# Two layers of a hybrid backbone on one core: opening on three queues, the last two items' rows added by 0/1 products, and expert gates applied to result rows

## The chip, the core and the metric

The kernel runs on one core of one Trainium2 chip: TensorE (PE) multiplies, VectorE (DVE) and ScalarE (ACT) work on tiles, GpSimd (POOL) and SyncE (SP) issue transfers, and so can ScalarE. 16 DMA engines move data between HBM and SBUF. The metric is the time of one execution on the device, in microseconds.

## What is computed

256 context rows and 256 latent rows of 1024 floats (f32) pass two layers; the output is the 256 latent rows, normed. The reference in short:

```python
for i in range(2):
    mod_l = split(silu(c) @ w_mod[i] + b_mod[i], 6)      # six vectors of 1024 for latent rows; mod_c for context rows
    u = modulated_norm(x, norm1_w[i], mod[0], mod[1]) @ w_in[i]
    y = token_mixers(u)                                  # SSD, Hyena long convolution, mLSTM, side by side
    x = x + mod[2] * (y @ w_out[i])
    x = x + mod[5] * hier_moe(modulated_norm(x, norm2_w[i], mod[3], mod[4]))
return rmsnorm(xl, final_norm_w)

def hier_moe(h):     # 4 groups of 8 experts: each row goes to 2 experts of its best group
    hid = silu(h @ w_gate[e]) * (h @ w_up[e]);  out += weight * (hid @ w_down[e])
```

Each expert has three matrices of 1 MB. In layer 1 only the latent rows go through the experts, in layer 0 all 512 rows.

## The kernel before

The program is one list of instructions per engine, written by hand; `due(name)` is the semaphore value at which a named step is done. x lies in SBUF as four tiles of 128 rows (0, 1 context, 2, 3 latent), PSUM has eight banks, given out in turn by `product`.

**Opening.** SP issues everything: the condition vectors and `ident`, the Hyena filter's parameters, then the weights of modulation in eight parts of 1 MB (three pairs, `first_pair`, and two single ones, `first_single`, numbers 6 and 7), x between them, the biases `b_mod`, the norm weights; then the in-projection's weights through a ring of four slots of 1 MB (`weight`), with `parameters(0)` (some 45 small loads), `router_parameters(0)` and constants in between. Modulation vectors 0 and 1 need parts 0 to 7: PE multiplies a part, ACT copies it to `grow`, PE transposes it (`mod_vector`), DVE sums it (`mod_columns`), then `modulators` writes `ab`. The filter of the Hyena convolution is made in six steps (`filter_step` 0 to 5) that stand between these. PE transposes the normed input (`input_columns`), ACT (context) and DVE (latent) scale it into `hT`, and the in-projection (`channel_major`, first "hy") starts when all of `hT` and the small columns (`pcol`) are there. The gates' product (`gate_sums`) comes after the six "hy" blocks.

**Experts.** Behind the router each expert's rows form items of up to 64 rows: 33 items in layer 0, 32 in layer 1. For item j, POOL gathers rows from DRAM (`rows`), PE transposes them (`gathered`), multiplies by gate and up (`gate_up`), ACT and DVE form the hidden rows, PE transposes (`hidden`) and multiplies (`down`). The 64x1024 result stands in one bank, the second half of its columns in partitions 64 to 127. In layer 0 ACT scales it by each row's weight (`weighted`) and the gate vector mod[5] is applied at the start of layer 1; in layer 1 DVE scales and gates it at once (`gated_halves`). POOL scatters it to `pair_rows` in DRAM, where each row of x has two places. Weights come to 17 (18) places of 1 MB (`expert_slots`), each reloaded when its matrix is used. A loop for more items (`flag != 0`) isn't entered with these inputs.

**Boundary.** All engines wait for each other (`stage_end`). SP waits for the last scatters and loads the pair rows of tiles 2, 3, 0, 1; DVE adds the two places (`pair_sum`), multiplies by the gate (`pair_gate`, layer 0) and adds to x (`pair_add`). Then come square (ACT), inverse (DVE), root (ACT), scaling, transposes and the in-projection of layer 1. Behind layer 1 the same sums lead to the output norm (`normed_output`).

## Time and profile before

| | |
|---|---|
| three runs | 1328.37, 1325.08, 1327.77 us; median 1327.77 |
| profiled execution | 1324.55 us, of which the span is 1322.6 us |
| PE busy | 1170.5 us (88%) |
| DVE, ACT, POOL busy | 605.8, 305.9, 133.2 us |
| DMA | 323.50 MB, mean 245 GB/s |

Times below are microseconds from the start of the span. Busy times of engines overlap, so shares don't add up to the whole. What counts is which engine or transfer the others wait for in a stretch.

### The profile page before, as it was taken

Reading aid. Unit: us, or ns where it says so; the run is one execution under the profiler, and the core shown is the slowest. Engines: PE = TensorE matmul, PEld = TensorE weight load, DVE = VectorE, ACT = ScalarE, POOL = GpSimd, SP = SyncE. Lnnn points to the kernel's source line nnn. Section 1 sums busy time; section 2 is a strip of 40 time slices with the busy share of each in tenths; the row PEclk is TensorE's granted clock in tenths of the full one; section 3 lists DMA queues with packets and bytes.
Section 4 is the critical chain, followed back from the end, with each engine's and each line's share of the span. In section 5 each row is a group of like instructions: output and inputs, shape, how many; then the busy total and the mean of one; then the engine's idle time right before and its main releaser. Section 6 shows DMA issues by size and latency. Waiting matters only on the chain. (4 is left out here: it accounts for less than half of the span.)

```text
span 1322.6 us, 19488 instructions
## 1 busy us (share of the span) xinstructions
PE 1170.5 (88%) x7596; PEld 769.2 (58%) x7596; DVE 605.8 (46%) x1233; ACT 305.9 (23%) x623; POOL 133.2 (10%) x144
## 2 busy tenths in 40 slices
PE   6799999999899979999877689998889899988882
PEld 3444547987678855555444466467768655545551
DVE  4424996037973641343111266973393533332223
ACT  4201112254552202131111233141442100000001
POOL 0000000000000012222221100000000112221220
PEclk9799999998999979999898899998999899998997
DMA  8653233236663579999999755441484879999982
GB/s 289 194 163 98 94 111 96 86 123 198 205 243 101 234 249 384 391 388 376 374 385 387 268 188 166 127 139 49 159 273 189 345 306 388 386 389 390 403 340 113
DMA packets 146965, 323.50 MB, mean 245 GB/s; under 512 B 28249, under 2 KB 111254, under 8 KB 121912
## 3 DMA queue, kind: packets, MB, share of 16 engines
q1 hardware_dynamic: 135384, 306.17, 63.8%
q0 software_dynamic: 11392, 15.79, 3.7%
q8 instruction: 63, 1.03, 0.3%
q14 instruction: 30, 0.25, 0.1%
q10 hardware_dynamic: 96, 0.26, 0.0%
HBM read 321.37 MB, written 22.28 MB: 260 GB/s over the span
## 5 line engine op out<-in xcount | busy, mean ns | idle before, releaser
L657 PE MATMUL bank<-hT,ring 128*128 128x512 f32 (+1 forms) x544 | 207.9, 540 | 1.8 <-DVE hT L1784 1.8
L657 PE MATMUL bank<-ring,hT 128*128 128x256 f32 (+1 forms) x928 | 180.3, 349 | 8.7 <-DVE chain L1794 3.9
L657 PEld LDWEIGHTS bank<-ring,hT 128*128 128x128 f32 x928 | 154.3, 194 | 27.8 <-issue 7.2
L657 PEld LDWEIGHTS bank<-hT,ring 128*128 128x128 f32 x544 | 104.5, 194 | 98.9 <-issue 91.9
L1788 DVE TENSOR_TENSOR ktok<-ktok,bank 64x256 f32<-64x256 f32 x65 | 27.5, 423 | 278.2 <-ACT ktok L1401 198.0
L657 PE MATMUL bank<-chain,qkT 128*64 128x256 f32 (+1 forms) x760 | 138.8, 380 | 6.1 <-DMA chain<-in_moe_w_up 2.7
L1401 ACT ACTIVATE ktok<-bank 64x256 f32<-64x256 f32 (+2 forms) x79 | 32.1, 406 | 346.9 <-PE bank L657 295.0
L657 PE MATMUL bank<-ring,qkT 128*64 128x256 f32 x512 | 92.7, 409 | 15.8 <-DMA ring<-in_moe_w_up 7.7
L1334 POOL DMA_INDIRECT pair_rows<-hyT,ysum x65 | 65.7, 1011 | 382.5 <-ACT hyT L1401 194.9
L657 PEld LDWEIGHTS bank<-chain,qkT 128*64 128x64 f32 (+1 forms) x760 | 82.6, 150 | 26.1 <-issue 4.8
L657 PEld LDWEIGHTS bank<-ring,qkT 128*64 128x64 f32 x512 | 56.3, 147 | 33.4 <-issue 15.1
L1401 ACT ACT_TABLE_LOAD x33 | 42.3, 1283 | 112.1 <-PE bank L657 68.5
L657 PE MATMUL bank<-big,qkT 128*64 128x256 f32 x256 | 60.3, 390 | 7.5 <-DMA chain<-in_moe_w_up 3.0
L1329 POOL DMA_INDIRECT big<-h_rows,ysum x65 | 61.7, 950 | 47.2 <-DVE ysum L1788 28.0
L1343 POOL DMA_DIRECT2D grow<-in_b_mod x4 | 2.3, 584 | 593.0 <-ACT grow L1401 593.0
L1214 PEld LDWEIGHTS bank<-ident,big 64*128 64x128 f32 x520 | 37.5, 140 | 37.3 <-issue 26.4
L657 PE MATMUL bank<-ident 128*128 128x256 f32 x188 | 51.4, 430 | 8.6 <-DMA hT<-pair_rows 7.7
L1794 DVE COPY qkT<-bank 128x512 f32<-128x512 f32 x65 | 45.0, 692 | 25.1 <-PE bank L1214 23.3
L1214 PE MATMUL bank<-ident,big 64*128 64x64 f32 x520 | 46.1, 229 | 9.8 <-DMA big<-h_rows,ysum 7.6
L657 PE MATMUL bank<-hT,qkT 128*64 128x256 f32 x256 | 51.0, 406 | 2.6 <-DMA hT<-in_moe_w_up 1.7
L1237 PEld LDWEIGHTS bank<-ident,ktok 64*128 64x128 f32 x130 | 20.3, 204 | 55.0 <-DVE qkT L1794 36.5
L1788 DVE TENSOR_TENSOR big<-big,bank 128x384 f32<-128x384 f32 x48 | 26.6, 554 | 55.5 <-ACT big L1401 52.1
(298 smaller groups left out, 1748.1 us busy)
## 6 DMA issues: line engine op xcount, KB each, us to landing
ring<-in_w_mod SPq DMA_DIRECT2D x40, 1024.0 KB
ring<-in_w_in SPq DMA_DIRECT2D x22, 1024.0 KB
chain<-in_moe_w_up SPq DMA_DIRECT2D x21, 1024.0 KB
chain<-in_moe_w_gate SPq DMA_DIRECT2D x19, 1024.0 KB
ring<-in_moe_w_down SPq DMA_DIRECT2D x18, 1024.0 KB
chain<-in_moe_w_down SPq DMA_DIRECT2D x17, 1024.0 KB
ring<-in_moe_w_gate SPq DMA_DIRECT2D x16, 1024.0 KB
ring<-in_moe_w_up SPq DMA_DIRECT2D x16, 1024.0 KB
```

Source lines behind the costliest of these rows:

```text
L657: return nc.tensor.matmul(o, a, b, start=s, stop=e, **k)
L1214: last = nc.tensor.transpose(b[:, k * R:(k + 1) * R], rows_v[r0:r0 + R, j % 2, k * P:(k + 1) * P], ident[r0:r0 + R, r0:r0 + R])
L1237: last = nc.tensor.transpose(b[:, f * R:(f + 1) * R], hid_v[0:R, j % 2, f::2], ident[0:R, 0:R])
L1329: return nc.gpsimd.indirect_dma_start(dst, None, h2_rows, bass.IndirectOffsetOnAxis(at_, 0), bounds_check=NT * P - 1, oob_is_err=False)
L1334: return nc.gpsimd.indirect_dma_start(pair_halves, bass.IndirectOffsetOnAxis(at_, 0), src, None, bounds_check=2 * MOST_PAIRS - 1, oob_is_e ...
L1343: pool.dma_start(modrow(m)[2:3, :], A["b_mod"][l:l + 1, m * D:(m + 1) * D]).then_inc(gate_bias_in[l][n], tick(f"gate_bias{l}{n}_in", ("gat ...
L1401: step(nc.scalar.activation(o, i, f, **k), *names)
L1788: step(V.tensor_tensor(o, a, b, op), *names)
L1794: step(V.tensor_copy(o, a), *names)
```

## The change

1. Opening on three queues. SP issues `ident`, the condition vectors, x, the eight parts and the in-projection's weights, nothing else. ACT issues the parameters of the filter's first steps. POOL issues the rest: 17 loads at once, and 38 after part 7 has been used. The small columns have their own semaphore (`prow`), and the "hy" block 0 waits for each k of `hT` apart. Filter steps 4 and 5 move behind the first two "hy" blocks.
2. Row gates. Layer 0's gate vector is applied to each item's result rows on DVE, by a row gate made of the context's and the latent rows' gate (two operations per item); `gate_rows(1)` stands in the router's stage in both layers; `pair_gate` and `weighted` are gone.
3. Late rows. The latent rows of the last two items are not scattered: PE adds them up into two banks per tile by a 0/1 matrix (`late`, `late_rows`), and DVE adds the banks to x (`pair_late`). So the pair rows of tiles 2 and 3 are loaded behind the scatter of the third-last item. The places in DRAM that aren't written are set to zero first (`zero_pairs`), and two of the weight places aren't reloaded late, as the pair rows are loaded there. `stage_end` behind the experts becomes a mark for each engine alone.

```diff
+LATE_ITEMS = 2
+PAIR_PLACES, LAST_IN_PAIRS = ((4, 5), (14, 4)), 80
 def taken_again(l, s, n):
+    if s in PAIR_PLACES[l] and n > LAST_IN_PAIRS:
+        return False
...
@@ SP @@
                 if l == 0:
-                    fetch("cond_in", cond_v[:, :, 0], A["c"][0].rearrange("(p k) -> p k", k=KB))
-                    fetch("cond_in", cond_v[:, :, 1], A["c_ctx"].rearrange("(p k) -> p k", k=KB))
-                    fetch("cond_in", ident[:, :], A["const_ident"])
-                    hidden_parameters(0)
-                    tap_parameters(0)
+                    fetch(sp, "cond_in", ident[:, :], A["const_ident"])
...
+                    fetch(sp, "x_in", x_v[:, 0:2, :], A["ctx"][0].rearrange("(t p) d -> p t d", p=P))
...
                     first_pair(0)
...
                     first_pair(1)
                     first_pair(2)
-                    fetch("dft_in", dft[:, :], A["const_dft"])
                     first_single(6)
-                    for layer in range(DEPTH):
-                        fetch("mod_bias_in", bmod_v[:, layer], A["b_mod"][layer].rearrange("(m p k) -> p m k", m=6, k=KB))
-                    norm_weights(0)
                     first_single(7)
...
+                if l:
+                    for t in (2, 3):
+                        sp.wait_ge(*due(("pairs", l - 1, t)))
+                zero_pairs(f"zeros{l}_in")
...
+                for n in (2, 1):
+                    sp.wait_ge(*due(("scattered", l, EXPERTS + EXTRA[l] - LATE_ITEMS - n)))
+                for t in (2, 3):
+                    sp.wait_ge(*due(last_in(PAIR_PLACES[l][t - 2])))
+                    sp.dma_start(two_v[l][t], pair_tiles[t]).then_inc(
+                        pairs_in[t], tick(f"pairs{t}_in", ("pairs", l, t), by=16))
...
-                for n in (1, 2):
-                    sp.wait_ge(*due(("scattered", l, EXPERTS + EXTRA[l] - n)))
...
+                if l + 1 < DEPTH:
+                    for n in (2, 1):
+                        sp.wait_ge(*due(("scattered", l, EXPERTS + EXTRA[l] - n)))
+                    for t in (0, 1):
+                        sp.dma_start(two_v[l][t], pair_tiles[t]).then_inc(
...
@@ PE @@
                         for k in range(KB):
+                            if (name, blk) == ("hy", 0):
+                                for s in range(1 if a0 else 0, 2):
+                                    pe.wait_ge(*due(("h1T", l, s, k)))
...
+                    if l == 0 and q == 0:
+                        pe.wait_ge(*due(("four",)))
+                        filter_step(l, 4)
+                        filter_step(l, 5)
...
-                if l:
-                    gate_rows(1)
+                gate_rows(1)
...
+                def late(t):
+
+                    b = [product(("late", l, t, half)) for half in range(2)]
+                    pe.wait_ge(*due(("late hot", l)))
+                    for n in range(LATE_ITEMS):
+                        j = items_now - LATE_ITEMS + n
+                        pe.wait_ge(*due(("result", l, j)))
+                        for half in range(2):
+                            rows = slice(R * half, R * half + R)
+                            last = mm(b[half][:, :], late_hot[l][rows, n, t - 2, :], res_v[rows, j % 2, :],
+                                      n == 0, n == LATE_ITEMS - 1)
...
@@ POOL @@
+            fetch(pool, "taps0_in", tcol[:, :], A["const_tcol"])
+            tap_parameters(pool, 0)
...
+            mod_biases(0)
+            norm_weights(pool, 0)
+            fetch(pool, "dft_in", dft[:, :], A["const_dft"])
+            parameters(pool, 0)
+            pool.wait_ge(*due(("made", ("mod", 0, 7))))
+            gate_parameters(pool, 0)
+            mod_biases(1)
...
+            router_parameters(pool, 0)
...
@@ DVE @@
-            def pair_gate(l, t):
-                two = two_v[l][t]
-                tt(two[:, 0, :], two[:, 0, :], grow_v[:, t // 2, :], MUL)
+            def pair_late(l, t):
+
+                dve.wait_ge(*due(("made", ("late", l, t))))
+                for half in range(2):
+                    cs_ = slice(512 * half, 512 * half + 512)
+                    tt(x_v[:, t, cs_], x_v[:, t, cs_], bank(("late", l, t, half))[:, :], ADD,
...
+                    if l and n == 0:
+                        step(V.memset(big[:, 0:2048], 0.0))
...
+                    ts(row_gate[:, j % 2, :], gate_halves[0], context_of[:, j:j + 1], None, MUL, None)
+                    stt(row_gate[:, j % 2, :], gate_halves[1], latent_of[:, j:j + 1], row_gate[:, j % 2, :], MUL, ADD)
...
+                    if l == 0:
+                        row_gates(j)
-                    if l and j:
+                    if j:
                         gated_halves(j - 1)
...
+                pair_sum(l, 2)
+                gated_halves(items_now - 1)
+                pair_add(l, 2)
+                pair_late(l, 2)
+                pair_sum(l, 3)
+                pair_add(l, 3)
+                pair_late(l, 3)
```

The order on PE in the opening, before: `four,ysum` is filter step 4, `tables` step 5, `xtok,condp` and `chain,condp` are parts 6 and 7, `ident,big` the transposes of the input, `hT,ring` the in-projection.

```order
L657 MATMUL bank<-hT,condp 32x256 x16
L657 MATMUL bank<-four,ysum 128x1 x4
L657 MATMUL bank<-qkT,tables 128x512 x2
L657 MATMUL bank<-hyT,tables 128x512 x2
L657 MATMUL bank<-xtok,condp 32x256 x8
L657 MATMUL bank<-chain,condp 32x256 x8
L688 MATMUL bank<-ident,grow 128x128 x8
L771 MATMUL bank<-ident,big 128x128 x32
L764 MATMUL bank<-ident,prow 128x78
L657 MATMUL bank<-hT,ring 128x512 x16
```

The same place in the changed program:

```order
L682 MATMUL bank<-xtok,condp 32x256 x8
L682 MATMUL bank<-chain,condp 32x256 x8
L713 MATMUL bank<-ident,grow 128x128 x8
L789 MATMUL bank<-ident,big 128x128 x32
L682 MATMUL bank<-hT,ring 128x512 x8
L782 MATMUL bank<-ident,prow 128x78
L682 MATMUL bank<-hT,ring 128x512 x8
L682 MATMUL bank<-ring,condp 32x256 x8
L682 MATMUL bank<-four,ysum 128x1 x4
L682 MATMUL bank<-qkT,tables 128x512 x2
L682 MATMUL bank<-hyT,tables 128x512 x2
L682 MATMUL bank<-hT,ring 128x512 x16
```

Steps 4 and 5 have moved from ahead of part 6 to behind the first two blocks of the in-projection, and the small columns (`ident,prow`) behind its first block.

DVE behind the last item of layer 1, before (`hyT<-bank,ysum,grow` is the scaled and gated result):

```order
L1788 TENSOR_TENSOR big<-big 128x1024
L1788 TENSOR_TENSOR x<-x,big 128x1024
L1788 TENSOR_TENSOR hT<-hT 128x1024
L1784 TENSOR_SCALAR small<-small 128x1
L1842 RECIPROCAL small<-small 128x1
L1788 TENSOR_TENSOR x<-x,hT 128x1024
L1791 SCALAR_TENSOR_TENSOR big<-x,small,ktok 128x1024
```

DVE there in the changed program:

```order
L1847 TENSOR_TENSOR big<-big 128x1024
L1850 SCALAR_TENSOR_TENSOR hyT<-bank,ysum,grow 128x512
L1847 TENSOR_TENSOR x<-x,big 128x1024
L1847 TENSOR_TENSOR x<-x,bank 128x512 x2
L1847 TENSOR_TENSOR hT<-hT 128x1024
L1847 TENSOR_TENSOR x<-x,hT 128x1024
L1847 TENSOR_TENSOR x<-x,bank 128x512 x2
```

The first sum of pair rows (`big<-big`) now stands ahead of the last item's result, each tile has two sums from banks more, and the inverse of tile 2 (`small`) comes behind all of them instead of behind the sum of tile 3.

## Rows read from the trace of the kernel before

**Rows 1.** Windows: busy us of each engine in the stretch, granted PE clock, DMA share, GB/s.

```profile
37.00:38.00 1.00, 1.00 (x8) 0.82 (x8) 0.93 (x3) 0.20 (x1) 0.00 (x0) 1.00 0.14 22
...
59.00:64.00 5.00, 4.86 (x7) 2.25 (x8) 0.24 (x1) 0.00 (x0) 0.00 (x0) 0.50 1.07 352
60.00:110.00 50.00, 50.00 (x162) 21.58 (x162) 14.14 (x19) 2.35 (x5) 0.00 (x0) 0.95 0.53 167
600.00:700.00 100.00, 84.58 (x586) 47.79 (x582) 21.02 (x42) 12.79 (x24) 22.98 (x24) 0.95 1.02 378
...
1294.00:1295.00 1.00, 1.00 (x13) 0.78 (x11) 0.00 (x0) 0.00 (x0) 0.00 (x0) 1.00 0.06 25
```

**Rows 2.** Timeline of SP's DMA issues, opening: start, duration, what is loaded.

```profile
24.69 10.01 SPq L401 DMA_DIRECT2D bmod<-in_b_mod  x2
...
37.54 0.55 SPq L482 DMA_DIRECT2D chain<-in_w_mod  x1
...
55.72 0.43 SPq L401 DMA_DIRECT2D rb<-in_exp_router_b  x1
```

**Rows 3.** Timeline of PE, opening: start, duration, operation, [idle before <-releaser].

```profile
36.63 1.05 PE L657 MATMUL bank<-four,ysum 128*128 128x1 f32 x8
...
41.15 1.07 PE L657 MATMUL bank<-xtok,condp 128*32 128x256 f32 x16
44.74 1.93 PE L657 MATMUL bank<-chain,condp 128*32 128x256 f32 x16 [2.52 <-DMA chain<-in_w_mod]
...
59.14 0.37 PE L764 MATMUL bank<-ident,prow 78*128 78x78 f32 x1 [5.18 <-DMA rb<-in_exp_router_b]
59.38 16.65 PE L657 MATMUL bank<-hT,ring 128*128 128x512 f32 x32
...
91.89 14.00 PE L657 MATMUL bank<-hT,ring 128*128 128x512 f32 x32
...
107.99 2.37 PE L657 MATMUL bank<-hT,tables 128*64 128x512 f32 x10
```

**Rows 4.** Timelines of PE, DVE, POOL and SP at the boundary of the layers.

```profile
742.30 1.94 PE L657 MATMUL bank<-big,ysum 128*64 128x512 f32 x8 [0.57 <-DVEq L1319]
...
767.81 8.83 PE L657 MATMUL bank<-hT,ring 128*128 128x256 f32 x32 [1.82 <-DVE hT L1784]
...
753.59 1.23 DVE L1788 TENSOR_TENSOR hT<-hT 128x1024 f32<-128x1024 f32 x1 [7.25 <-DMA hT<-pair_rows]
...
735.84 1.00 POOL L1334 DMA_INDIRECT pair_rows<-hyT,ysum  x1 [6.85 <-ACT hyT L1401]
...
748.61 0.91 SPq L628 DMA_DIRECT2D hT<-pair_rows  x2
```

**Rows 5.** Timelines of PE, DVE and POOL at the end of the span.

```profile
1298.48 1.94 PE L657 MATMUL bank<-hT,ysum 128*64 128x512 f32 x8 [0.98 <-DVE ysum L1794]
...
1300.55 0.75 DVE L1791 SCALAR_TENSOR_TENSOR hyT<-bank,ysum,grow 128x512 f32<-128x512 f32 x1 [2.22 <-PEq L668]
...
1317.80 1.28 DVE L1791 SCALAR_TENSOR_TENSOR big<-x,small,ktok 128x1024 f32<-128x1024 f32 x1 [0.77 <-ACT small L1401]
...
1291.81 1.00 POOL L1334 DMA_INDIRECT pair_rows<-hyT,ysum  x1 [5.86 <-DVE ysum L1794]
```

**Rows 6.** Timeline of DVE, opening: the latent half of the scaled input.

```profile
50.23 6.18 DVE L1784 TENSOR_SCALAR hT<-bank,ab 128x256 f32<-128x256 f32 x8
```

**Rows 7.** Groups of POOL by line: busy us, mean ns, idle before.

```profile
L1347 POOL DMA_DIRECT2D h_rows<-big x6 | 3.3, 544 | 146.9 <-ACT big L1401 146.9
```

**Rows 8.** Timeline of PE in the router's stages of layers 0 and 1.

```profile
465.89 1.09 PE L657 MATMUL bank<-qkT,hyT 128*128 128x47 f32 x8 [0.38 <-DVE qkT L1788]
...
1040.87 1.08 PE L657 MATMUL bank<-grow,gate_four 128*64 128x512 f32 x4
```

**Rows 9.** Landings of scatters issued in 600:700, and of the one in 1291:1292.5.

```profile
DMA to landing us min/median/max: 6.8/7.3/8.1
...
DMA to landing us min/median/max: 3.9/3.9/3.9
```

More of the change, by code:

```diff
@@ L182, in build @@
         consts_in, x_in, norm_in, out_written = sem("consts_in"), sem("x_in"), sem("norm_in"), sem("out_written")
+        prow_in = [sem(f"prow{l}_in") for l in range(DEPTH)]
         params_in = [sem(f"params{l}_in") for l in range(DEPTH)]
@@ L197, in build @@
         more_rows_out = [sem(f"more_rows{l}_out") for l in range(DEPTH)]
+        zeros_in = [sem(f"zeros{l}_in") for l in range(DEPTH)]
+        more_zeros = [sem(f"more_zeros{l}_in") for l in range(DEPTH)]
+        more_pairs = [sem(f"more_pairs{l}_in") for l in range(DEPTH)]
+        more_sums = [sem(f"more_sums{l}") for l in range(DEPTH)]
         more_weights = [sem(f"more_weights{l}_in") for l in range(DEPTH)]
@@ L225, in build @@
         rw = sb("rw", KB * 36)
+        steps = sb("steps", 72)
         rb = sb("rb", 36)
@@ L601, in _, with last_in @@
                     sp.wait_ge(*due(("more table", l)))
-                    fetch("norm_in", final_w, A["final_norm_w"].partition_broadcast(P))
+                    fetch(sp, "norm_in", final_w, A["final_norm_w"].partition_broadcast(P))
+                def last_in(s):
+                    return ("used", ("expert", l, max(n for n in range(matrices) if places[n] == s)))
+                for n in (2, 1):
[4 more added lines that the diff above has]
+                        pairs_in[t], tick(f"pairs{t}_in", ("pairs", l, t), by=16))
                 if l + 1 < DEPTH:
@@ L1271, in _ @@
                 down(items_now - 1)
-                stage_end(l, "moe")
+                for t in (2, 3):
+                    late(t)
+                pe.drain().then_inc(pe_done, tick("pe_done", ("end", "pe", l, "moe")))
                 with pe.If(flag != 0):
+                    pe.wait_ge(*due(("end", "act", l, "moe")))
+                    pe.wait_ge(*due(("end", "dve", l, "moe")))
                     pe.nop().then_inc(more_pe[l], 1)
@@ L1357, in rows @@
                         rows_in[j % 4], tick(f"rows{j % 4}_in", ("rows", l, j), by=16))
+                pool.wait_ge(*due((f"zeros{l}_in",)))
                 for j in range(AHEAD):
@@ L1478, in _ @@
                     act.wait_ge(*due(("ab", l, 0)))
-                    for k in range(0, KB, 2):
-                        input_columns(k, 1, ("h1T", l, 1, "act"))
+                    for blk in (0, 2):
+                        name = ("h1", l, blk, 1)
+                        act.wait_ge(*due(("made", name)))
+                        for k in (2 * blk, 2 * blk + 1):
+                            names = [("read", name)] if k % 2 else []
+                            fn(hT_v[:, k, L:2 * L], bank(name)[:, 256 * (k % 2):256 * (k % 2) + L], ACT.Identity, *names,
+                               ("h1T", l, 1, k), scale=ab_v[:, 0, k, 0:1], bias=ab_v[:, 1, k, 0:1])
                     input_squares(0)
@@ L1914, in _ @@
                     step(V.memset(vaug[:, :], 1.0))
-                    for n in (1, 2, 3):
-                        filter_step(l, n)
+                    filter_step(l, 1)
+                    inverse(l, 0, NT)
+                    filter_step(l, 2)
                 def normed_input(t):
```

401 lines of the change are left out of this document (214 added, 187 removed).

## Prediction

> **What bounds the kernel now.** I read the windows first. In the window from 60 to 110 us PE is busy for 50.00 of 50 us [rows 1]: once the in-projection runs, PE is the bound and nothing beside it costs time. In the window from 600 to 700 PE is busy for 84.58 us, while the DMA engines stand at a share of 1.02 and 378 GB/s [rows 1]: a mixture-of-experts stage is bound by its 3 MB of weights per item (3.15 MB / 378 GB/s = 8.3 us), and VectorE with 21.02 us has room. Three places are left where neither is full, and the change works at them.
>
> The opening: SP issues everything. The two bias loads hold it for 10.01 us from 24.69, so weight part 7, the last that the first norm's modulators need, is issued only at 37.54 [rows 2]; between 37 and 38 us the DMA engines move 22 GB/s [rows 1]. PE takes part 7 at 44.74, and the in-projection starts at 59.38, behind a wait of 5.18 us that ends with the router's bias, issued at 55.72 as the last of some 50 small parameters [rows 2, 3].
>
> The boundary of the layers: the last product of the last item starts at 742.30 and takes 1.94, so ends at T = 744.24; in-projection of layer 1 starts at 767.81 [rows 4], 23.6 us later. Between them lie the scaled result, its scatter, the load of the pair rows (issued at 748.61, awaited by VectorE until 753.59, so 5.0 us), and sums of 1.23 us.
>
> The end: the last product starts at 1298.48 and ends at T' = 1300.42; the output norm's last operation starts at 1317.80 [rows 5], and the span ends at 1322.6, 22.2 us after T'.
>
> **The change, part by part.**
>
> *Opening, gain.* SP now issues three small loads (about 0.7 us each), the five of x, then the weight parts with nothing between them. Up to the end of part 7 these are 8.4 MB of parts, 2.1 MB of x, and beside them about 1.1 MB on the other two queues (filter weights, decays, the Fourier table). 11.6 MB at 378 to 390 GB/s are 30 to 31 us; they can flow from about 5 us, so part 7 is there at 36, and PE takes it at about 36.5 instead of 44.74: 8.2 earlier. From there to the modulators it took 5.5 us (44.74 to the first use at 50.23 [rows 3, 6]); I keep it, so 42.1. Next, before, PE waited until all 16 blocks of the normed input were scaled and then for the parameters: 59.38 - 50.23 = 9.15. Now each product waits for its own k, and the parameters aren't asked for. But PE must first issue 32 transposes into 8 banks, two for each k, and VectorE frees a pair of banks every 6.18 / 8 = 0.77 us [rows 6]; so it can start after about five of them, 3.9 us. In-projection then starts at 46.0: 13.4 earlier.
>
> *Opening, cost.* Filter steps 4 and 5 stood where PE waited for part 6 (from 36.63 to 41.15, so 4.5 us [rows 3]). They now stand behind the first hyena weights, in the stretch where PE is full: -4.5, uncovered. VectorE's part of them (two copies and four sums) lies under products of 7 us each. The transpose of the small columns is only moved. The first 32 rows of in-projection took 16.65 us where later ones took 14.00 [rows 3], and from 59 to 64 us the granted clock was 0.50 [rows 1], that is 1.2 GHz, after PE had waited. Now there is no wait of 5 us ahead of them, but there are shorter ones; I take half of the 2.65 us, +1.3. Sum of the opening: 13.4 - 4.5 + 1.3 = **10.2**. Since PE is full from here on, it passes on. The weight stream of the experts restarts when PE frees places, so it shifts with PE too.
>
> *The POOL queue.* 38 of the moved loads are issued after part 7 has been used (about 38 us), and the gate product, which ran at 107.99 [rows 3], waits for the last. It would now run at about 107.99 - 59.38 + 46.0 + 4.5 = 99. The trace has direct POOL DMAs of 544 ns [rows 7] and indirect ones of 1.00 us [rows 4]; with 0.3 between them, a guess, the 38 end at 70 at 0.84 each and at 87 at 1.3. Hidden. If each also waited out a VectorE operation of 0.77 us [rows 6], they would end at 38 + 38 x 1.61 = 99, just at the need; from there on the sum loses what they are late, which is the slower rival below. The Trainium skill, page "SBUF — State Buffer", section "SBUF: two separate sides", speaks against the move: while VectorE runs an operation that takes both shared ports, GpSimd can't write the descriptors of its DMAs. No row here shows it. By the page's "A bandwidth-pool intuition that's wrong (but worth ruling out)" such a DMA takes about 3.1 us in place of 0.62; an estimate by that figure has the 38 end at 156, and the time 57 us longer.
>
> *Router of layer 0.* The row gates move from item 4 of the experts (off the bound, gain nothing) to behind the ranks. Four rows of this kind took 1.08 us in layer 1 [rows 8]; here it is eight, 2.1 us, ahead of 14 filler products that just filled the gap: the pair products waited 0.38 [rows 8]. So they start 1.7 later; the second half waited for VectorE anyway and makes up 0.4: **-1.3**. In layer 1 a zeroing of 2048 columns stands in a wait of VectorE for a square: **-0.3**.
>
> *Experts.* In layer 0, three operations of 128x512 per item go to VectorE (two for the row gate, one for the scaled result), bounded by the 0.75 us of such a one in layer 1 [rows 5]: 2.3 us more per item of 8, on an engine with 21.02 busy of 100 us [rows 1]. The copy that PE needs next (rows of j + 1) comes ahead of them. 0. Two places less for the last loads leave them 11 or more matrices ahead, over 25 us at 2.8 each: 0. The zeros (2 MB read, 2 MB written per layer) go out behind the in-projection weights, where the DMA share was 0.53 [rows 1] and less: 0.
>
> *Boundary.* The load of pair rows for tiles 2 and 3 now waits only for the scatters up to item 30. That of item 30 is issued at about 736.3 (before 735.84 [rows 4]); landing took 3.9 us for one near the end of a stream and 7.3 in the median at full stream [rows 9]. So SP goes on at 740.2 to 743.6, and with 5.0 us for the load, tile 2 is there at 745.2 to 748.6; I take T + 2. VectorE waits for it ahead of the last scaled result: sum 1.25, result 0.8 (T + 4.0), add 1.25, the 0/1 products meanwhile 1.2, two bank adds 1.45: tile 2 is whole at T + 6.7. Tile 3: sum, add, two bank adds, 4.0: T + 10.7, and behind it the rest of VectorE's prologue and the inverse, T + 12.0. Root and scaling on ScalarE 1.4, square of tile 3 1.25, inverse and root 0.8, scaling 0.75, transposes and first block 1.4: T + 17.6, where it was 23.6. The first block is paced by its k blocks, 0.5: **+5.5** (3.1 with the late landing, 6.5 with the early one).
>
> *End.* The scatter of item 29 was issued at 1291.81 [rows 5] and landed after 3.9 [rows 9]: SP issues the loads at 1295.8, tile 2 is there at 1300.7. Sum 1302.0, result 1302.8, add 1304.0, bank adds 1305.5, tile 3 1309.5, inverse 1310.3, table load and root 1.5, output norm of tile 2 to 1313.1; square, inverse and root of tile 3 by 1313.9; its norm starts at 1314.4, where it was 1317.80: **+3.4**.
>
> Sum: 10.2 - 1.6 + 5.5 + 3.4 = **17.5**. The profiled execution took 1324.55, so 1307.1 in its terms. That execution lies 3.2 below the median of the three runs (1327.77) and 0.5 below the lowest; against the median it is 1310.3. I predict 1310.
>
> **The rivals.**
>
> *Pair rows come late.* The chain of the last results now holds the load in front of them. If scatters land after 7.3 us and the two loads of layer 0 stand behind stragglers of the weight stream, boundary gives 2 and the end 1: 1316. For it: the landing rows. Against it: from 1294 to 1295 the DMA engines were nearly idle, 25 GB/s [rows 1]. 15%.
>
> *The POOL queue holds the gate product; slower.* Place: ahead of the gate sums of layer 0, PE waits for the 38 loads, five of which have 768 or 1024 short pieces. It starts to cost at (99 - 38) / 38 = 1.6 us each and eats the whole gain at (99 + 17.5 - 38) / 38 = 2.1. At 2.5 it is 133 - 99 = 34 late: 1344. For it: such short pieces appear on POOL in no row, and SP's two bias loads held it 5 us each. Against it: all POOL rows are at 0.5 to 1.0, and SP's were held by a full queue. 9%, of which slower 5, the same 2.
>
> *The stream gives it back.* If the experts' weights aren't earlier by what PE is (their order, slow single engines, scatters of VectorE's results later), the opening's gain is halved and more: 1318 to 1324. Against it: the engines are idle before the stage's first item. 8%, of which the same 3.
>
> *It is worth more.* Clock high throughout the opening, pair rows there before T: 1302. 8%.
>
> *The forecast*: 60%. Its own range is 1305 to 1316. To hold 8 in 10 the range takes in late pair rows and the better case, 1301 to 1320; the queue and most of the stream case stay out. Faster by over 0.3% (4 us, about what a measurement of this kernel can tell from no change): 0.90; within it 0.05; slower 0.05.
>
> **What would show it.** In the changed profile: part 7 taken by PE at 36 to 37.5; in-projection from 45 to 48; filter steps 4 and 5 as 4.5 us behind the first two hyena blocks; no wait of PE ahead of the gate sums (the POOL queue's last parameter before 99); T earlier by 8 to 10; 16 to 19 us from T to the in-projection of layer 1; 18 to 20 from T' to the end. The prediction is wrong if the gate sums wait, if VectorE's wait for pair rows ends more than 4 us behind T, or if the experts' stage is longer than before.

## The result, and the profile after

The changed kernel takes 1309.61 us (median of four runs, 1306.41 to 1313.21) against 1328.07 before (1325.08 to 1330.06): ratio 0.9863, 95% interval [0.9843, 0.9884]. The profiled execution took 1306.41 us, its span is 1304.6. Run again on another chip, the same kernel took 1312.97 (1311.01 to 1318.88) against 1327.42: 0.9900 [0.9877, 0.9923]. Its executions on the two chips spread over 12 us (1306.4 to 1318.9), which matters below.

First the opening: windows of the changed kernel (columns as in [rows 1]), then SP's DMA issues, then TensorE.

```profile
37.00:38.00 1.00, 0.00 (x0) 0.00 (x0) 0.94 (x2) 0.00 (x0) 0.00 (x0) 1.00 1.09 347
...
59.00:64.00 5.00, 5.00 (x32) 2.49 (x31) 2.49 (x4) 0.38 (x1) 1.78 (x3) 1.00 0.63 117
...
600.00:700.00 100.00, 80.75 (x548) 47.00 (x548) 40.83 (x74) 4.00 (x11) 21.49 (x22) 0.91 1.02 383
```

```profile
16.55 5.29 SPq L495 DMA_DIRECT2D xtok<-in_w_mod  x1
21.89 5.30 SPq L495 DMA_DIRECT2D chain<-in_w_mod  x1
```

```profile
38.33 1.07 PE L682 MATMUL bank<-chain,condp 128*32 128x256 f32 x16 [1.94 <-DMA chain<-in_w_mod]
...
46.22 7.03 PE L682 MATMUL bank<-hT,ring 128*128 128x512 f32 x16
53.09 0.23 PE L782 MATMUL bank<-ident,prow 78*128 78x78 f32 x1
...
61.16 1.05 PE L682 MATMUL bank<-four,ysum 128*128 128x1 f32 x8
62.08 1.96 PE L682 MATMUL bank<-qkT,tables 128*128 128x512 f32 x4
63.88 1.88 PE L682 MATMUL bank<-hyT,tables 128*128 128x512 f32 x4
...
96.51 3.65 PE L682 MATMUL bank<-hT,tables 128*64 128x512 f32 x16
```

Between 37 and 38 us the DMA engines are full (347 GB/s, 22 before in [rows 1]): the last weight part is on its way, with loads for the in-projection behind it. SP had issued that part by 27.2 instead of 38.1. TensorE takes it at 38.33 (44.74 in [rows 3]), and the in-projection starts at 46.22 (59.38). Its first 16 products take 7.03 us, the full rate: nothing is lost to the clock, while 32 took 16.65 before [rows 3]. Steps 4 and 5 stand behind the first two blocks, from 61.16 to the next product at 65.60: 4.4 us. The gate product runs at 96.51, 11.5 earlier, and no wait stands in its row. In 600 to 700 VectorE is busy for 40.83 of 100 us instead of 21.02, and the stream of weights stays at 383 GB/s (378 before).

The boundary: TensorE, VectorE, then SP.

```profile
728.19 1.94 PE L682 MATMUL bank<-big,ysum 128*64 128x512 f32 x8 [1.52 <-DVE ysum L1853]
730.06 3.86 PE L682 MATMUL bank<-hyT,ktok 64*128 64x512 f32 x16
...
744.93 8.12 PE L682 MATMUL bank<-hT,ring 128*128 128x256 f32 x32
...
757.35 3.57 PE L789 MATMUL bank<-ident,big 128*128 128x128 f32 x16 [3.30 <-DVE big L1844]
```

```profile
728.95 1.23 DVE L1847 TENSOR_TENSOR hT<-hT 128x1024 f32<-128x1024 f32 x1 [0.90 <-DMA hT<-pair_rows]
730.27 0.75 DVE L1850 SCALAR_TENSOR_TENSOR hyT<-bank,ysum,grow 128x512 f32<-128x512 f32 x1
...
736.28 1.41 DVE L1847 TENSOR_TENSOR x<-x,bank 128x512 f32<-128x512 f32 x2
```

```profile
724.04 0.90 SPq L624 DMA_DIRECT2D hT<-pair_rows  x2
```

T is 728.19 + 1.94 = 730.13 (744.24 before). VectorE's sum of tile 2's pair rows starts at 728.95, 1.2 ahead of T; before, that load landed at 753.59, 9.35 behind T [rows 4]. The in-projection of layer 1 starts at 744.93, T + 14.8 (T + 23.6 before). Behind it is a wait of 3.30 us for the scaled tile 1 (2.01 before), which no step of mine had named.

The end:

```profile
1284.33 1.94 PE L682 MATMUL bank<-ring,ysum 128*64 128x512 f32 x8 [0.99 <-DVE ysum L1853]
...
1286.18 1.23 DVE L1847 TENSOR_TENSOR big<-big 128x1024 f32<-128x1024 f32 x1 [1.99 <-DMA big<-pair_rows]
```

```profile
1295.99 1.28 ACT L1461 ACT_TABLE_LOAD   x1 [3.56 <-DVE small L1906]
```

```profile
1297.62 1.28 DVE L1850 SCALAR_TENSOR_TENSOR big<-x,small,ktok 128x1024 f32<-128x1024 f32 x1 [1.71 <-ACT small L1461]
...
1299.69 1.28 DVE L1850 SCALAR_TENSOR_TENSOR big<-x,small,ktok 128x1024 f32<-128x1024 f32 x1 [0.40 <-ACT small L1461]
```

T' is 1286.27, the last norm starts at 1299.69, the end is T' + 18.3 (22.2 before).

**Where the time went, stage by stage.** All from TensorE's timeline, each entry the difference of two starts in us (T, T' and the end of the span are ends). The "rank product" is the first one of the router's `ranks`; T' is in layer 1 what T is in layer 0. The second column is the changed kernel in its first profile, the third the same kernel profiled again; the others are experiments told below (late rows undone; rotation of banks moved by four).

| stretch | before | after | after again | late undone | banks +4 |
|---|---|---|---|---|---|
| start to in-projection | 59.38 | 46.22 | 46.31 | 46.00 | 46.90 |
| to gate sums | 48.61 | 50.29 | 50.29 | 50.29 | 50.28 |
| to layer 0's rank product | 335.68 | 333.16 | 337.73 | 336.93 | 336.86 |
| to the first expert transposes | 32.82 | 32.85 | 32.47 | 32.47 | 31.52 |
| to T | 267.75 | 267.61 | 269.78 | 269.78 | 268.87 |
| T to in-projection, layer 1 | 23.57 | 14.80 | 14.79 | 21.10 | 15.54 |
| to gate sums | 30.70 | 32.60 | 32.51 | 32.69 | 32.44 |
| to the transposes behind the scan | 187.99 | 194.13 | 194.03 | 187.94 | 187.81 |
| to layer 1's rank product | 53.37 | 54.72 | 54.71 | 54.47 | 54.34 |
| to T' | 260.55 | 259.89 | 260.72 | 259.85 | 259.52 |
| T' to the end | 22.18 | 18.33 | 19.16 | 23.68 | 18.42 |

Three entries were not foreseen. The stretch to layer 0's rank product is 2.5 shorter after, but 2.1 longer than before in the second execution of the same kernel. And layer 1 gives back 8.7 of the 8.8 that the boundary gained: 1.9 up to its gate sums, 1.35 ahead of its rank product, and 6.1 in the scan, less 0.66 in the experts.

### The profile page after: what moved, and what is told of

Read it like the earlier page. It is cut to its first block and busy times, and to the rows that moved or that the text cites. A ratio compares the mean times of both kernels' runs of the same rounds, so it can differ in the third digit from the quotient of the medians.

```text
span 1304.6 us, 19602 instructions
## 1 busy us (share of the span) xinstructions
PE 1169.4 (90%) x7608; PEld 767.7 (59%) x7608; DVE 677.2 (52%) x1348; ACT 281.8 (22%) x588; POOL 161.6 (12%) x196
## 5 line engine op out<-in xcount | busy, mean ns | idle before, releaser
L682 PE MATMUL bank<-hT,ring 128*128 128x512 f32 (+1 forms) x544 | 204.4, 533 | 0.0
L682 PE MATMUL bank<-chain,qkT 128*64 128x256 f32 (+1 forms) x744 | 143.2, 388 | 16.3 <-DMA x<-in_moe_w_up 5.0
L682 PE MATMUL bank<-ring,qkT 128*64 128x256 f32 x544 | 96.5, 393 | 13.4 <-DMA hT<-in_moe_w_up 4.2
L1850 DVE SCALAR_TENSOR_TENSOR hyT<-bank,ysum,grow 128x512 f32<-128x512 f32 x65 | 48.8, 751 | 29.8 <-PE bank L682 28.5
```

The lines of the kernel that those rows point to most:

```text
L682: return nc.tensor.matmul(o, a, b, start=s, stop=e, **k)
L1850: step(V.scalar_tensor_tensor(o, a, s, b, op0, op1), *names)
```

## Experiments

The changed kernel itself and three with one part undone ran side by side on one chip. The later ones ran on two other chips; the kernel before took 1327.42, 1328.24 and 1327.03 on the three, so it differed by 0.8 us from chip to chip. Ratios are against the kernel before.

**The changed kernel again.** No edit.

> The changed kernel once more, nothing edited. In its first profile three readings need an explanation: the part from the gate sums to layer 0's rank product was 2.5 us shorter than before, the part from layer 1's in-projection to its last expert 8.7 us longer, and in both stretches rows appear with doubled durations (granted clock under 1.00) at places where the other kernel has none. Theory A, chance: the clock falls now here, now there behind the mixer's short waits; this execution then shows the doubled rows elsewhere, while all waits are the same to 0.1 us, and the whole moves by a few us (1306 to 1314). Theory B, caused by the change: the same rows between 912 and 945 us are doubled again, and none between 285 and 300. Both expect the gate sums at 96.5 and the in-projection of layer 1 at 14.8 us behind the last product of layer 0.

Measured: 1312.97. In layer 1 the stretch takes 194.03 again (Theory B). In layer 0 it is chance: windows of the same place, 188.5 us behind the gate sums, in the first and the second execution:

```profile
285.00:300.00 15.00, 13.47 (x162) 10.82 (x159) 9.54 (x22) 10.23 (x27) 0.00 (x0) 1.00 0.85 280
```

```profile
285.00:300.00 15.00, 13.48 (x128) 10.51 (x127) 7.35 (x18) 7.60 (x20) 0.00 (x0) 0.77 0.63 206
```

The busy time is equal, but at a granted clock of 0.77 instead of 1.00 TensorE gets through 128 products, not 162; the kernel before shows 0.77 there too (296.75 to 311.75). So 2.5 to 4.6 us of the first profile's gain are luck. In the twelve other profiles of the changed kernel and its variants the stretch takes 334.13 to 337.97, so 333.16 is the rare value; of the kernel before there is one profile (335.68), which can't tell what is usual there.

**The queues undone.** SP issues all loads in the old order; steps 4 and 5 stay in their new place.

```diff
+                        if (l, name, q) == (0, "hy", 0):
+                            parameters(sp, 0)
+                            gate_parameters(sp, 0)
+                            router_parameters(sp, 0)
...
+                    hidden_parameters(sp, 0)
...
+                    tap_parameters(sp, 0)
+                    first_pair(0)
...
                     first_single(6)
+                    for i in range(DEPTH):
+                        fetch(sp, f"mod_bias{i}_in", bmod_v[:, i], A["b_mod"][i].rearrange("(m p k) -> p m k", m=6, k=KB))
+                    norm_weights(sp, 0)
                     first_single(7)
...
-            tap_parameters(pool, 0)
...
-            gate_parameters(pool, 0)
```

> Only the three queues are undone: SP issues every load in the old order, everything else as changed, filter steps 4 and 5 still behind the first two hyena blocks. My theory (SP's 10 us on the two bias loads and the x loads behind the first pair hold part 7): part 7 is taken near 44.7 instead of 38.3, the in-projection starts 6.4 later, at 52.6, nothing waits for the router's parameters, and the time is 1309.6 + 6.4 = 1316. Rival 1, the queues carry the whole opening: the small columns or the gate sums wait for their parameters as well, in-projection near 59, time 1322. Rival 2, given back later: no slower than the changed kernel by more than 2.

Measured: 1317.01, 4.0 more than the changed kernel; ratio 0.9924 [0.9904, 0.9945]. SP's issues, then TensorE, then ScalarE:

```profile
26.92 8.65 SPq L400 DMA_DIRECT2D bmod<-in_b_mod  x2
...
38.40 0.55 SPq L495 DMA_DIRECT2D chain<-in_w_mod  x1
```

```profile
30.02 7.19 PE L698 MATMUL bank<-ktok,ysum 64*128 64x512 f32 x8 [11.78 <-ACT ysum L1462]
...
46.81 1.07 PE L698 MATMUL bank<-chain,condp 128*32 128x256 f32 x16
```

```profile
24.83 1.06 ACT L1462 ACTIVATE chain<-x 128x1024 f32<-128x1024 f32 x1 [12.57 <-DMA x<-in_x]
```

Part 7 is issued at 38.40 as before and lands 5.6 later, at about 44, but TensorE takes it at 46.81 without a wait. What holds it is something else: the changed kernel has ScalarE square x ahead of the filter's second activation, and with the old order x comes behind the first pair of parts. ScalarE waits for it until 24.83, TensorE for ScalarE until 30.02, and its next eight products take 7.19 at a granted clock of 0.50 (3.71 in the changed kernel). So this run isn't the old opening: only some 6 of the 8.5 us by which part 7 is used later (46.81, 38.33 in the changed kernel) can be put down to SP's order. In-projection starts at 54.39 and the gate sums at 104.68, 8.1 later where 6.4 was expected. Nothing else waits for SP: the router's bias, issued as late as 57.68, holds nothing any more. Of the 8.1, 2.8 are left at T' and 4.0 in the medians. The layer 0 stretch that varies by chance was 334.13 here, which accounts for 3.6 of what is missing at T'.

**Steps 4 and 5 back ahead of part 6.**

```diff
                     filter_step(l, 3)
+                    pe.wait_ge(*due(("four",)))
+                    filter_step(l, 4)
+                    filter_step(l, 5)
                     modulation(l, 6)
...
-                    if l == 0 and q == 0:
-                        pe.wait_ge(*due(("four",)))
-                        filter_step(l, 4)
-                        filter_step(l, 5)
```

> Only filter steps 4 and 5 stand again ahead of parts 6 and 7, on TensorE and VectorE; the queues stay three. My theory: their cover was SP's lateness and is gone with it. Their input (VectorE's four sums) is ready at 38.7 only, so part 6 goes from 35.3 to about 42.6, the in-projection starts about 5.3 later and the 4.4 us behind the first hyena blocks are saved: 0.9 slower, 1310.5. Rival: the steps find cover in the waits of TensorE (1.9 us ahead of part 7) and all 4.4 are saved: 1305.

Measured: 1314.75, 1.8 more, within the spread. TensorE there:

```profile
38.94 1.02 PE L682 MATMUL bank<-four,ysum 128*128 128x1 f32 x8 [0.97 <-DVE ysum L1852]
41.84 2.38 PE L682 MATMUL bank<-qkT,tables 128*128 128x512 f32 x4 [1.88 <-DVE qkT L1846]
44.01 3.20 PE L682 MATMUL bank<-hyT,tables 128*128 128x512 f32 x4
47.14 1.07 PE L682 MATMUL bank<-xtok,condp 128*32 128x256 f32 x16
```

The steps wait for VectorE and hold parts 6 and 7; in-projection at 55.33, gate sums at 101.28, 4.7 later (0.9 was expected: I had left out the waits and the low clock, 3.20 for four products that take 1.88 above). So the steps find no cover there any more, and the rival falls. That the move pays in the time isn't shown: T' came 1.4 sooner in this profile than in the changed kernel's second, each of five later stretches being shorter by 0.8 to 1.6.

**The late rows undone.**

```diff
-LATE_ITEMS = 2
+LATE_ITEMS = 0
...
-                for t in (2, 3):
-                    late(t)
...
+                gated_halves(items_now - 1)
                 pair_sum(l, 2)
-                gated_halves(items_now - 1)
                 pair_add(l, 2)
-                pair_late(l, 2)
```

> Only the late rows are undone: all results are scattered, the pair rows of tiles 2 and 3 are loaded behind the last scatter, no 0/1 products and no sums from banks. The gates on result rows, the prologue split in two, and the opening stay. My theory: the chain result, scatter, landing, load comes back, 8.8 us at the boundary less the two gate products (1.5) and the sums from banks (2.8, which are gone), so about 6, and 3.9 at the end: 1309.6 + 10 = 1320. Rival: the boundary's gain came from the gates and the order of the prologue, and the late rows give only the end's 4: 1314.

Measured: 1315.94, only 3.0 more. In the table the boundary is 6.3 longer and the end 4.5, as expected (6 and 4); yet the scan of layer 1, some 200 us away from both, takes 187.94 instead of 194.03. The late rows cost 6.1 us there.

What links them is `product`, which gives out the eight PSUM banks in turn. Some products of the scan ask for a fixed bank (the states `st` for bank 4), the others take the next of the rotation. Up to that mixer the changed kernel asks four times more for late products, twice less for gate rows and four times less for the prologue's blocks, so it starts two banks off (v of tile 0 in bank 5, not 7; with the late rows undone in 1). In the kernel before, v of tile 2 falls on bank 4 and waits for the state's reader. In the changed one the x tokens of tile 2 do. Timelines of TensorE in the scan, before and after:

```profile
902.75 13.25 PE L657 MATMUL bank<-ring,hT 128*128 128x256 f32 x64 [3.88 <-DVE chain L1794]
...
936.06 0.94 PE L657 MATMUL bank<-qkT 64*128 64x128 f32 x12
...
940.05 0.39 PE L657 MATMUL bank<-mask,ident 128*128 128x512 bf16 x1 [2.83 <-ACT big L1401]
...
941.42 5.50 PE L657 MATMUL bank<-ring,hT 128*128 128x256 f32 x32
```

```profile
891.99 0.66 PE L912 MATMUL bank<-ident,chain 128*128 128x128 f32 x4 [2.51 <-DVE chain L1853]
...
912.40 0.94 PE L682 MATMUL bank<-qkT 64*128 64x128 f32 x12 [1.04 <-ACT chain L1461]
...
915.28 0.61 PE L682 MATMUL bank<-mask,ident 128*128 128x512 bf16 x1 [1.72 <-ACT big L1461]
...
919.26 8.09 PE L682 MATMUL bank<-ring,hT 128*128 128x256 f32 x32 [1.44 <-DVE big L1847]
```

A wait of 3.88 has become one of 2.51, and one of 2.83 three of 1.04, 1.72 and 1.44 close together. Among these the clock falls (0.61 for the row that takes 0.39): the same 32 products take 8.09 instead of 5.50. (Behind the 3.88 it fell too: 64 products took 13.25, 10.74 in the changed kernel.) The larger loss comes right behind, where the waits are the same in both kernels, 1.34 and 1.47 us before, 1.33 and 1.47 after; the stretch as a window, before and changed:

```profile
946.86:960.14 13.28, 10.48 (x136) 7.77 (x136) 6.01 (x12) 8.24 (x17) 0.00 (x0) 1.00 0.75 239
```

```profile
927.27:945.31 18.04, 15.24 (x136) 10.99 (x136) 7.47 (x14) 8.23 (x17) 0.00 (x0) 0.72 0.53 176
```

The same 136 products take 4.8 us more at 0.72 instead of 1.00. The second execution of the changed kernel has 18.04 there as well; with the late rows undone it is 13.28.

**The rotation moved, alone.** To test that, the changed kernel got these two lines, and the same with 4.

```diff
+                if l:
+                    turn[0] += 2
```

> The changed kernel with the rotation of PSUM banks moved on by two at the start of layer 1 and nothing else. The changed kernel issues, behind layer 0's router, two products from the rotation less-than-a-round apart from before, so that layer 1's mixer uses other banks: the product of v of tile 0 has bank 5 there, bank 7 in the kernel before, bank 1 where the late rows are undone. From layer 1's gate sums to the transposes behind its scan it took 194.1 and 194.0 us in two executions of the changed kernel, 188.0 before and 187.9 with the late rows undone. Theory A, banks: which product waits for which bank's reader in the scan decides, and with it where TensorE goes idle and its clock falls; with the banks of before this stretch takes 188 again, and the time falls by 6 from 1313 to 1307. Theory B: the stretch depends on the late rows themselves or on when loads arrive; it stays 194, and the time the same.

> The same with the rotation moved on by four, which gives layer 1 the banks it has where the late rows are undone (v of tile 0 in bank 1). Theory A, banks: the stretch from the gate sums to the transposes behind the scan takes 188 as there, and the time is 1307; its waits stand at the places they have in that kernel (0.93 and 1.92 us). Theory B: 194 and no change.

Measured: 1305.30 (0.9831 [0.9818, 0.9845]) and 1304.19 (0.9820 [0.9799, 0.9841]); the stretch takes 188.51 and 187.81, and the window of 18.04 is 13.28 in both. Theory A holds for the stretch; the medians are 7.7 and 8.8 under the changed kernel's 1312.97 and 4.3 and 5.4 under its first 1309.61, where 6 was expected. The stretch as one window, before, changed, and changed with the rotation moved by four:

```profile
798.51:986.50 187.99, 173.78 (x1155) 122.82 (x1155) 120.95 (x238) 62.01 (x124) 1.10 (x2) 0.98 0.46 143
```

```profile
777.53:971.66 194.13, 179.82 (x1155) 126.68 (x1155) 120.94 (x238) 61.97 (x124) 1.09 (x2) 0.95 0.46 149
```

```profile
782.41:970.22 187.81, 174.73 (x1156) 123.32 (x1155) 120.97 (x238) 61.97 (x124) 1.09 (x2) 0.98 0.49 154
```

The same products, and TensorE idle for 14.2, 14.3 and 13.1 us. The 6 us are all in its busy time, at a granted clock of 0.95 instead of 0.98. So the banks did not add waiting; they moved some waits, and with them the places where the clock falls, the largest of which is behind two waits that didn't move. The Trainium skill, page "TensorE: Matmul & The Clock Gate", section "A second HAM failure mode: psum-queue depth-cycling", tells of a kernel whose short idle times between groups, from cycling through banks, make the clock go down and up. The trace agrees as far as that: the granted clock falls behind waits of 1.04 to 1.72 us and rises again.

**Two orders on VectorE in layer 1.**

```diff
-                    conv("hy", blk, hy_v, 20, 38, 6, t0 // 2, *([("hy z", l, 0)] if blk == 1 else []))
                     if l and blk == 0:
                         inverse(l, 1, 1)
                         dve.wait_ge(*due(("rstd", l, 1, 1)))
                         normed_input(1)
+                    conv("hy", blk, hy_v, 20, 38, 6, t0 // 2, *([("hy z", l, 0)] if blk == 1 else []))
...
-                    if l and n == 0:
-                        step(V.memset(big[:, 0:2048], 0.0))
...
                     normed_columns(t)
+                    if l and n == 0:
+                        step(V.memset(big[:, 0:2048], 0.0))
```

> Two places on VectorE in layer 1: the inverse and scaling of tile 1 stand ahead of the first block's convolution instead of behind it, and the zeroing of 2048 columns behind the first tile's columns instead of ahead of its norm. Theory: these are the two new waits of the changed kernel, 3.3 us ahead of the context transposes (of which the convolution is 1.6 and its order 0.8) and 0.75 in the router; both go, the in-projection's second pair starts 2.0 to 2.4 earlier and the router 0.75, and the time falls by 3. Rival: what is saved is taken by the clock or by waits in the scan, and the time is the same within 1.

Measured: 1308.24 (0.9851 [0.9829, 0.9872]). The wait of 3.30 is 1.42:

```profile
760.45 0.80 PE L789 MATMUL bank<-ident,big 128*128 128x128 f32 x5 [1.42 <-DVE big L1844]
```

In-projection to gate sums takes 31.28 (32.51), but that isn't the edit's: the last four of the transposes now wait 1.13 for the convolution behind it, and two profiles without the edit (steps 4 and 5 back, ninety more loads) have 31.28 and 31.29, since the 16 transposes take 2.24 there and not 3.47. The router's wait of 0.73 is gone, but its stretch stays (54.69), at a granted clock of 0.91 instead of 0.94, and the scan took 195.96. So by stretches nothing is gained up to the rank product, as the rival has it. The median is 1.4 to 4.7 lower; in the profile T' came 2.9 sooner behind the first transposes, which no edit touches.

**The inverse and the table at both ends.** The edited kernel leaves out the case of more items than `EXPERTS + EXTRA`, a branch that isn't entered with these inputs.

```diff
+            fn(small[:, 41:42], small[:, 42:43], ACT.Sqrt)
             for t in range(2, NT):
...
-                    inverse(l, 2, 1)
...
                 pair_sum(l, 3)
+                inverse(l + 1, 2, 1)
                 pair_add(l, 3)
...
-            inverse(DEPTH, 2, 1)
```

> The inverse of tile 2 stands ahead of tile 3's last two sums at both ends, and the square root's table is loaded behind the last expert's silu. With more items than experts this would be wrong; with these inputs that branch isn't entered. Theory: at the boundary ScalarE scales tile 2 while VectorE sums tile 3, so its square of tile 3 isn't held up by 2.6 us: in-projection of layer 1 at 12.6 us behind the last product of layer 0 instead of 14.8; at the end the last norm starts 1.8 earlier and the 1.28 of the table load lie under the sums: 16.8 instead of 18.3 to 19.2. Time lower by 4. Rival: VectorE's chain of sums (pair rows of two tiles, 6.6 us) bounds both places, and 1 is gained at each at most.

Measured: 1309.61 (0.9853 [0.9831, 0.9874]). T to in-projection takes 12.21 instead of 14.79, as expected, but the stretch behind it 34.07 instead of 32.51, since the context tiles come no sooner; the end takes 17.33 instead of 19.16 (18.33 in the first profile). Hence 1 kept of 2.6 at the boundary, and 1 to 1.8 at the end.

**Ninety more loads in POOL's queue.**

```diff
             pool.wait_ge(*due(("made", ("mod", 0, 7))))
+            for n in range(90):
+                fetch(pool, "params0_in", spare[0:HEADS, n:n + 1], A["ssd_dt_bias"][0, 0].unsqueeze(1))
             gate_parameters(pool, 0)
```

> GpSimd's queue issues 90 more small loads (six floats each, into a spare tile) ahead of the 38 that follow part 7; the gate product waits for all 128. By 0.50 us each, what such loads measured in the changed kernel while VectorE and ScalarE were busy beside them, the 128 end at 39.7 + 21.1 + 45 = 105.8 and have landed at about 108, where the gate product stood at 96.6: a wait of 11 us, and 1313 + 11 = 1324. That would be the price at which the queue becomes the bound, (96.6 - 39.7 - 2) / 0.55 = 100 loads. Rival: loads cost more when more of them stand in the queue or while VectorE works (3.1 us each as a page of the Trainium skill has it): the wait is over 100 us. Rival 2: what is late there is caught up by TensorE later, since the experts' weights come at their own pace: under 1318.

Measured: 1326.07 (0.9991 [0.9974, 1.0008]), so the whole gain. POOL, TensorE, and the window:

```profile
39.65 44.86 POOL L401 DMA_DIRECT2D spare<-in_ssd_dt_bias  x90 [29.41 <-PE bank L683]
...
105.19 0.55 POOL L401 DMA_DIRECT2D rb<-in_exp_router_b  x1
```

```profile
110.68 4.90 PE L683 MATMUL bank<-hT,tables 128*64 128x512 f32 x12 [13.95 <-DMA rb<-in_exp_router_b]
```

```profile
40.00:85.00 45.00, 44.94 (x164) 23.36 (x165) 20.57 (x33) 5.29 (x10) 45.00 (x91) 0.96 0.47 139
```

A load costs 44.86 / 90 = 0.50 us while VectorE is busy for 20.57 of 45 us. The Trainium skill, page "SBUF — State Buffer", section "A bandwidth-pool intuition that's wrong (but worth ruling out)", has about 3.1 for one that overlaps a `tensor_copy` on VectorE. No load here shows it; whether such a copy ran beside one isn't shown either. The gate product waits 13.95 us (11 expected: the last load landed 4.9 behind the end of its issue, not 2). Most of what is late there stays late: 14.1 at the gate sums, 9.3 at T' (against the second profile), 13.1 in the medians.

**Each row gate made twice**, in layer 0.

```diff
                     if l == 0:
                         row_gates(j)
+                        row_gates(j)
```

> Each of layer 0's row gates is made twice (the same two operations of 128x512, with the same result): 1.25 us more of VectorE for each of 33 items. Theory: VectorE has room, the copy that TensorE waits for stands ahead of them, and the stage stays at 267.6 to 269.8 us from the first transposes to the last down product; time as the changed kernel's, 1310 to 1313. Rival: the two operations lie between the hidden rows and what TensorE needs next, so that doubling adds up to 1.25 us per item, 41 us, or a part of it; then the single ones cost something too.

Measured: 1314.55 (0.9914 [0.9889, 0.9939]). The stage takes 271.09, where the kernels without it took 267.3 to 269.8: 1.3 to 3.8 us for 41 us more of VectorE, 0.8 of them a last product at the lower clock (2.71 for 1.94). Nearly all of it is hidden.

**The three edits together**, with the rotation moved by four and by two.

> The three edits together: PSUM rotation moved on by four in layer 1, tile 1's norm ahead of the first convolution and the zeroing behind the first tile's columns, tile 2's inverse ahead of tile 3's last sums with the root's table loaded early. With the rotation by four alone it was 1304.2; the boundary gives 2.6, the wait ahead of the context transposes 2.5, the router 0.8, the end 1.4, less about 1 that they share: 1298. Rival: with other arrival times in the scan the clock falls there again as in the changed kernel (194 us where it should be 188), and it is 1304.

> The same three edits with the rotation moved on by two. By the run with that offset alone (1305.3) it should be 1299; the scan's stretch 188.5. Rival as for the other: 1305, the stretch 194.

Measured: 1301.17 (0.9801 [0.9779, 0.9823]) and 1301.86 (0.9803 [0.9777, 0.9829]), some 3 us above the expectations, and 3.0 and 3.4 below the rotation moved alone. The scan takes 186.38 and 188.75, and the end 16.76 and 17.29. What fails is the boundary: 15.83 and 15.52 instead of 12.21. TensorE with the rotation moved by four, and with the ends' edit alone:

```profile
742.29 5.23 PE L682 MATMUL bank<-ident 128*128 128x256 f32 x12 [3.51 <-DVEq L2659]
747.36 1.94 PE L806 MATMUL bank<-ident,big 128*128 128x128 f32 x16
```

```profile
741.20 2.83 PE L682 MATMUL bank<-ident 128*128 128x256 f32 x12
743.87 1.06 PE L804 MATMUL bank<-ident,big 128*128 128x128 f32 x8
```

The rotation is moved ahead of the prologue, so its filler products, and behind them the transposes, now ask for a bank that a late product of tile 3 still holds: the wait ends with VectorE's last work on that tile. With the rotation moved and nothing else the boundary takes 15.54 and 15.97 instead of 14.79, so the move costs 0.8 and 1.2 there too. Moving the rotation behind the prologue's blocks wasn't tried.

## Why the prediction was right, and where only by luck

1310.3 was the sum and 1309.61 the first measurement, 1312.97 the second. The sum's parts, 17.5 in all, against the first profile, whose span is 18.0 shorter:

| term | predicted | measured |
|---|---|---|
| in-projection of layer 0 sooner | 13.4 | 13.2 |
| filter steps 4 and 5 | -4.5 | -4.4 |
| clock behind the start | +1.3 | +2.65 |
| router of layer 0 | -1.3 | 0 (-2.5 and +2.5) |
| boundary | +5.5 | +8.8 |
| layer 1, memset and the rest | -0.3 | -8.7 (memset about -1.0) |
| end | +3.4 | +3.9 (3.0 in the second profile) |
| not in the sum: chance in layer 0 | 0 | +2.5, or -2.1 in the second profile |

- **Opening: right** in place, and in size because two steps cancel. Part 7 was taken at 38.33 and not at 36.5, after a wait of 1.94 for its load; from there to the first product it was 7.9 us and not 9.5. The moved steps' price held. The clock's half was too careful: all of 2.65 came back.
- **POOL's queue: right.** The 38 loads ended at 60.78, 36 us ahead of the gate product. Ninety more show that a longer queue does hold it, but by the number of loads; the 1.6 to 2.5 us each of the slower rival appear nowhere (0.50 to 0.92).
- **Router of layer 0: the step right, its size and what it left out not.** The row gates took 3.2 us and not 2.1, and the gather of the first rows began 2.5 later behind the rank product than before (29.5, 27.0). But from there to the first expert transposes it was 3.4 us instead of 5.9; the DMA engines were busy for 0.39 of that time, 0.83 before. The sum had no term for the gather.
- **Experts: right** in the first profile (267.6 against 267.75). In the others of the changed kernel and its variants the stage takes 267.3 to 269.8; what makes up to 2 us more is open.
- **Boundary: mechanism right, size low by 3.3.** The failing step is "tile 2 is there at 745.2 to 748.6; I take T + 2". It was there at T - 1.2. The scatter of item 30 left 8.8 ahead of T where I had 7.9, and it landed in about 2.6 us (2.6 in the second profile too), at the stream's end, where T + 2 took 4.9 and the rows had 3.9 and 7.3. Of the 8.8 the late rows carry 6.3; 2.5 is what stays with them undone (gates on result rows, split prologue, marks in place of `stage_end`).
- **Layer 1: wrong.** "Experts 0" and "memset -0.3" left out all between. The bank rotation costs 6.1. Up to the gate sums 1.9 is lost: the context transposes start 0.6 later, behind the wait for tile 1's norm, and take 3.57 instead of 2.24, which not every profile shows. The zeroing costs about 1.0: with the rotation by four the stretch to the rank product takes 54.34, with the zeroing moved as well 53.34. Of the rivals "the stream gives it back" has the right size and the wrong place: the stream gave back nothing, most of it was TensorE's clock.
- **End: right** within the spread, in the first profile again by two errors that cancel: the scatter of item 29 left 7.3 ahead of T' and not 8.6, and landed in 2.4 and not 3.9. In the second it was 8.6 and 3.9, as in the rows.

So the sum was right by luck: 8.4 lost in layer 1 beyond the forecast met 3.3 at the boundary, 1.35 of clock, 1.3 of router, 0.5 at the end and 2.5 of chance. Two of its own signs say so: T came 14.1 sooner (7.7 in the second profile), where 8 to 10 was forecast, and the boundary took 14.8, where 16 to 19 was. With the rotation moved back by two, the same change took 1305.3.

What stays open: why delays at the gate sums shrink on the way, from 8.1 to 2.8 at T' with the queues undone and from 4.7 to less than nothing with steps 4 and 5 back (in part chance in layer 0), and what decides at a given wait whether the clock falls.

## What to carry to other kernels

When a change adds or drops a buffer request anywhere, the buffers of everything behind it shift. Where some requests in a rotation are fixed, list who collides with them before and after, even stages away; a line that moves the rotation back is worth a run. A kernel with one part undone is a new kernel, too: look for waits that neither of the others has before you read its time. And compare stages one by one, on at least two executions of the same kernel: a total that comes out as forecast can hide 9 us of loss and 9 of gain.

## What the runs showed of the hardware

- Direct loads issued by GpSimd cost its queue 0.50 to 0.57 us each with VectorE busy for 20.57 of 45 us, 0.84 to 0.92 with 768 or 1024 short pieces. SP's two bias loads held it 8.65 to 10.01 us behind megabyte loads; parts 6 and 7, 1 MB each, held it 5.3 each in the changed kernel.
- Equal idle time of TensorE (14.2 and 14.3 us in 188 to 194) came with a granted clock of 0.98 or 0.95. Waits of 2.83 or of 1.04, 1.72 and 1.44 came first; behind the next two, 1.3 and 1.5 in both kernels, 136 products ran at 1.00 in 13.28 us or at 0.72 in 18.04.
- At one wait of 1.49 us in layer 0 the clock fell to 1.2 GHz in one execution and not in the other, 2.5 to 4.6 us apart.
- At the end of a weight stream a scatter of result rows landed in 2.6 us in layer 0, twice, and in 2.4 and 3.9 in layer 1; inside a stream it took 7.3 in the median [rows 9].
